# Second feed-forward layer of a two-layer diffusion block: its up projection as seven block products

## The chip, the cores and the metric

The kernel runs on one core of a Trainium2 chip. The metric is the device time of one execution in microseconds (us), the median of several. One core has a matrix engine (TensorE: PE for the products, PEld for the loading of its weights), a vector engine (VectorE, DVE), an activation engine (ScalarE, ACT), a general engine (GpSimd, POOL) and a queue engine that starts most transfers (SyncE, SP). Each runs its own program in order; they meet at semaphores.

## The reference

Two blocks, each a mixer and a gated convolutional feed-forward layer (FFN), on 1024 latent tokens and 256 context tokens of width 1024 in float32. What the change touches is the FFN of the second block, on the 1024 latent tokens alone:

```
def conv_ffn(h, w_up, conv_w, conv_b, w_down):
    gate, val = jnp.split(dwconv_centred(h @ w_up, conv_w, conv_b), 2, axis=-1)
    return (jax.nn.silu(gate) * val) @ w_down
...
xl = xl + g2 * conv_ffn(rmsnorm(xl, norm_ffn_w[i]) * (1 + sc2) + sh2, ffn_w_up[i], ...)
```

The convolution runs over three neighbouring tokens, each channel for itself. The hidden width is 2816, so `w_up` is 1024 x 5632 and `w_down` 2816 x 1024.

## The kernel before

Channels lie on the 128 partitions, tokens along the row. The hidden width is cut into FT = 22 tiles of 128 channels. One tile has a gate half and a value half; for each, 8 weight blocks of 128x128 (the width 1024 = KD x 128) are multiplied with 1024 tokens in two groups of 512. Every float32 product is made of three passes (`split_passes`, high x high, high x low, low x high), for which each operand is split into a rounded part (`_hi`) and a remainder (`_lo`). So one tile has 2 x 2 x 8 x 3 = 96 matmuls of 512 columns for the up projection, and its down projection has ND = 16 pieces (8 output blocks x 2 token groups) of 3 matmuls, 48 more.

The function `ffn` writes an order by hand for each engine; nothing is scheduled by a planner:

- SP loads the two halves of a tile's up weights (`up_raw`) and its down weights (`dn_raw`), 512 KB each.
- POOL splits them: `up_hi` (L1285) and `up_lo` (L1288) for each half, then `dn_hi` (L1294) and `dn_lo` (L1297), on 128x1024 each, two operands in the on-chip memory SBUF for the `_lo`.
- PE (L1317 for up, L1310 for down) runs the up products of tile f, and between them the down pieces of tile f-1, at steps given by a list `place`. A gate half fills banks 0 and 1 of the accumulators (PSUM), a value half banks 3 and 4; down pieces alternate between banks 6 and 7.
- ACT takes a half out of PSUM with the middle tap (`centre`, L1366), DVE adds the two outer taps (L1395, L1401), ACT applies Silu (L1376), DVE multiplies the halves (L1433), ACT rounds the product (`act_hi`, L1380) and DVE makes the remainder (`act_lo`, L1435).
- DVE adds each down piece to the residual (`add`, L1414). PE may begin piece j when the add of piece j-2 has ended, since there are two banks.

Ahead of the tiles `normalise` makes the normed activations: DVE multiplies by the inverse root (L279), ACT scales and shifts and rounds, and DVE makes the remainder (L288), eight blocks of 128x1024 each. PE's first tile takes each block as soon as it is there. The order of DVE inside a tile, and the down pieces on PE:

```
        def body(dve, f, s, with_down):
            if with_down:
                for j in range(in_gate):
                    add(f - 1, j)
            dve.wait_ge(lo_set, f + 1)
            convolve(f, 0)
            if with_down:
                for j in range(in_gate, ND):
                    add(f - 1, j)
            convolve(f, 1)
            ...
```

## Time and profile before

| what | value |
|---|---|
| median of 3 runs (lowest to highest) | 3511.73 us (3507.72 to 3512.95) |
| the profiled execution | 3508.97 us, its span on the core 3507.2 us |
| PE busy, share of the span | 3208.5 us, 91% |
| DVE, ACT, POOL busy | 2204.2, 984.5, 988.9 us |
| chain that ended last, largest parts | PE L1317 14%, PE L1310 7% of the span |
| L1317, three passes, both FFN layers | 652.9, 652.2 and 650.5 us busy, 1760 matmuls each |
| up weights, issue to landing | 88 transfers of 512 KB, median 3.5 us |

The span is the time from the first to the last instruction of the profiled execution; 1.8 us of its time lie around it. Busy time is the sum of the durations of an engine's instructions, and it includes time in which an instruction that has begun is held up. The second FFN fills the last fifth of the span.

### The profile page before, as it was taken

Reading aid. Unit: us, or ns where it says so; the run is one execution under the profiler, and the core shown is the slowest. Engines: PE = TensorE matmul, PEld = TensorE weight load, DVE = VectorE, ACT = ScalarE, POOL = GpSimd, SP = SyncE. Lnnn points to the kernel's source line nnn. Section 1 sums busy time; section 2 is a strip of 40 time slices with the busy share of each in tenths; the row PEclk is TensorE's granted clock in tenths of the full one; section 3 lists DMA queues with packets and bytes.
Section 4 is the critical chain, followed back from the end, with each engine's and each line's share of the span. In section 5 each row is a group of like instructions: output and inputs, shape, how many; then the busy total and the mean of one; then the engine's idle time right before and its main releaser. Section 6 shows DMA issues by size and latency. Waiting matters only on the chain. (4 is left out here: it accounts for less than half of the span.)

```text
span 3507.2 us, 53513 instructions
## 1 busy us (share of the span) xinstructions
PE 3208.5 (91%) x20022; PEld 2673.9 (76%) x20022; DVE 2204.2 (63%) x2995; ACT 984.5 (28%) x1504; POOL 988.9 (28%) x715
## 2 busy tenths in 40 slices
PE   5989988886899999999996879999998799999998
PEld 3879956665688888888885658878887688888886
DVE  7976067886366666666666256666663566666666
ACT  4111245544131111111112434444442312112111
POOL 1322145551222222222220032221212333333331
PEclk8999999998999999999998879999999899999999
DMA  4558120004111111111100200000002111111111
GB/s 194 193 177 292 68 77 2 2 2 158 38 47 38 36 37 40 36 36 36 36 30 14 72 9 5 5 6 10 2 13 84 55 42 54 48 42 54 48 46 56
DMA packets 64267, 196.35 MB, mean 56 GB/s; under 512 B 7680, under 2 KB 20864, under 8 KB 62848
## 3 DMA queue, kind: packets, MB, share of 16 engines
q1 hardware_dynamic: 47280, 163.83, 14.0%
q10 hardware_dynamic: 16848, 30.56, 2.6%
q8 instruction: 100, 1.64, 0.2%
q14 instruction: 39, 0.32, 0.0%
HBM read 175.49 MB, written 18.87 MB: 55 GB/s over the span
## 5 line engine op out<-in xcount | busy, mean ns | idle before, releaser
L1414 DVE SCALAR_TENSOR_TENSOR resid<-ps,mod,resid 128x512 f32<-128x512 f32 (+1 forms) x880 | 601.8, 697 | 471.5 <-PE ps L1310 471.3
L1317 PE MATMUL ps<-hf_hi,up_hi 128*128 128x512 f32 (+1 forms) x1760 | 652.9, 371 | 31.3 <-DVE hf_lo L288 22.3
L1317 PE MATMUL ps<-hf_lo,up_hi 128*128 128x512 f32 (+1 forms) x1760 | 652.2, 371 | 0.0
L1317 PE MATMUL ps<-hf_hi,up_lo 128*128 128x512 f32 (+1 forms) x1760 | 650.5, 370 | 0.0
L1285 POOL TENSOR_SCALAR up_hi<-up_raw 128x1024 fp32r<-128x1024 f32 x88 | 94.7, 1076 | 1161.0 <-PE ps L1317 1099.4
L1317 PEld LDWEIGHTS ps<-hf_hi,up_hi 128*128 128x128 f32 x1760 | 334.6, 190 | 87.6 <-issue 34.3
L1317 PEld LDWEIGHTS ps<-hf_hi,up_lo 128*128 128x128 f32 x1760 | 334.2, 190 | 56.5
L1317 PEld LDWEIGHTS ps<-hf_lo,up_hi 128*128 128x128 f32 x1760 | 334.8, 190 | 51.6
L1310 PE MATMUL ps<-act_hi,dn_hi 128*128 128x512 f32 (+1 forms) x880 | 333.1, 379 | 18.3 <-DVE act_lo L1435 16.1
L1366 ACT ACTIVATE conv<-ps,conv_w 128x1280 f32<-128x1280 f32 (+1 forms) x88 | 115.7, 1315 | 802.3 <-PE ps L1317 802.0
L1310 PE MATMUL ps<-act_lo,dn_hi 128*128 128x512 f32 (+1 forms) x880 | 326.7, 371 | 0.0
L1310 PE MATMUL ps<-act_hi,dn_lo 128*128 128x512 f32 (+1 forms) x880 | 325.6, 370 | 0.0
L820 POOL TENSOR_TENSOR k_decayed<-decay,qk 128x256 f32<-128x256 f32 (+1 forms) x240 | 194.1, 838 | 193.1 <-ACT decay L985 193.1
L131 DVE CUSTOM_DVE_ANT_0 ps<-adaw_ring,cond,adab 128x1024 f32<-128x1024 f32 x128 | 205.9, 1608 | 58.9 <-DMA adaw_ring<-in_adaw 48.5
L1310 PEld LDWEIGHTS ps<-act_hi,dn_hi 128*128 128x128 f32 x880 | 166.4, 189 | 71.0 <-DVE resid L1414 20.7
L1288 POOL TENSOR_TENSOR up_lo<-up_raw,up_hi 128x1024 fp32r<-128x1024 f32 x88 | 213.2, 2423 | 7.3
L2080 DVE TENSOR_TENSOR pt_lo<-ps,pt_hi 128x512 fp32r<-128x512 f32 (+1 forms) x192 | 114.5, 597 | 135.4 <-ACT pt_hi L1981 134.8
L1310 PEld LDWEIGHTS ps<-act_lo,dn_hi 128*128 128x128 f32 x880 | 166.9, 190 | 28.6
L1310 PEld LDWEIGHTS ps<-act_hi,dn_lo 128*128 128x128 f32 x880 | 166.5, 189 | 28.8
L649 PE MATMUL ps<-wvr_hi,h_hi 128*128 128x256 f32 x640 | 182.5, 285 | 4.2 <-ACTq L678 4.2
L649 PE MATMUL ps<-wvr_lo,h_hi 128*128 128x256 f32 x640 | 182.1, 284 | 0.0
L649 PE MATMUL ps<-wvr_hi,h_lo 128*128 128x256 f32 x640 | 182.0, 284 | 0.0
(239 smaller groups left out, 6590.5 us busy)
## 6 DMA issues: line engine op xcount, KB each, us to landing
up_raw<-in_up SPq DMA_DIRECT2D x88, 512.0 KB, 3.5
adaw_ring<-in_adaw SPq DMA_DIRECT2D x80, 512.0 KB, 4.0
dn_raw<-in_dn SPq DMA_DIRECT2D x44, 512.0 KB, 3.5
vr<-vr_out ACTq DMA_DIRECT2D x80, 128.0 KB, 3.7
adaw_first<-in_adaw SPq DMA_DIRECT2D x16, 512.0 KB, 21.8
wvr_raw<-in_wvr SPq DMA_DIRECT2D x8, 1024.0 KB, 7.3
x<-in_xT ACTq DMA_DIRECT2D x8, 640.0 KB, 16.9
r<-vr ACTq DMA_DIRECT2D x10, 512.0 KB, 3.8
```

The source lines that it names most:

```text
L131: return dve.tensor_tensor_reduce(junk, w, self.cond[:, j, :], 1.0, self.bias[:, n:n + 1], ALU.mult, ALU.add, self.c.mod[:, n, j:j + 1])
L649: mm = pe.matmul(c.ps[:, u % RING, 0:W], a[:, k, t * P:(t + 1) * P], b[:, s, k, :], start=(k == 0 and a is h_hi and b is w_hi), stop=(k == ...
L820: pool.tensor_tensor(kd[u % 2][:, lo * P:hi * P].rearrange("p (b t) -> p b t", t=P), e[:, u % 2, (LEVEL + lo) * P:(LEVEL + hi) * P].rearra ...
L1285: pool.tensor_scalar(up_hi[:, half, :, :], up_raw[:, half, :, :], 1.0, 1.0, ALU.mult, ALU.mult).then_inc(up_hi_set, 1)
L1288: pool.tensor_tensor(up_lo[:, half, :, :], up_raw[:, half, :, :], up_hi[:, half, :, :].bitcast(F32), ALU.subtract).then_inc(up_split, 1)
L1310: mm = pe.matmul(c.ps[:, 6 + j % 2, 0:w], a[:, s, m * P:(m + 1) * P], b[:, s, t:t + w], start=(a is dn_hi and b is act_hi), stop=(a is dn_lo))
L1317: mm = pe.matmul(c.psf[:, at:at + w], a[:, half, k, :], b[:, k, t:t + w], start=(k == 0 and a is up_hi and b is h_hi), stop=(k == KD - 1 a ...
L1366: act.activation(y[:, half, span], u(half), ACT.Identity, scale=cw[:, bass.ds(f * 8 + (half * 4 + 1), 1)], bias=cw[:, bass.ds(f * 8 + (hal ...
L1414: dve.scalar_tensor_tensor(resid[:, m, t:t + w], c.ps[:, 6 + j % 2, 0:w], c.mod[:, gate + m, cond[t]:cond[t] + 1], resid[:, m, t:t + w], A ...
L2080: dve.tensor_tensor(pt_lo[:, k0:k0 + w, at], c.psf[:, T_PS[n]:T_PS[n] + w * P].rearrange("p (k t) -> p k t", t=P), pt_hi[:, k0:k0 + w, at] ...
```

## The change

The second FFN no longer calls `normalise` and `ffn`, but a function of its own, `seven_ffn`. The first FFN stays. The up projection of one tile is seen as a 2 x 2 block matrix of weights (gate and value half, times the first and second half of the 1024 input channels, HK = 4 blocks each) times a 2 x 2 block matrix of activations (halves of the channels times halves of the tokens, HALF = 512). Strassen's identity in Winograd's form makes the four output blocks from seven block products in place of eight, from four weight sums, four activation differences and seven sums of products:

- the operands of the seven products of the activations (`x_hi`, `x_lo`, 128 x 7 x 4 x 512) are made once ahead of the tiles: DVE scales (`scale`, 16 instructions), POOL takes differences (`differences`, 16 instructions), ACT rounds and DVE makes the remainders (`low`, 28 instructions);
- for each tile POOL makes four sums of weight blocks and splits seven operands of 128x512 into a ring of three places (`slots`); it splits operand n when the product three before has ended. The split of the down weights stands after the third operand, and there is one place for it where there were two;
- PE runs seven products of 4 x 3 matmuls (84 in place of 96) into banks 4, 0, 5, 3, 1, 4, 2, and the down pieces of the tile before at the steps 13 to 20 and 24 to 27 of 28;
- DVE makes seven sums of products in PSUM or SBUF (`mixed`), between the adds and the taps, and begins a tile with the value half of the tile before (`value`).

The core of the diff (declarations, the SP queue, the norm on ACT and the last tile are left out):

```diff
+HALF = SEQ // 2
+HK = KD // 2
+SEVEN_BANKS = (4, 0, 5, 3, 1, 4, 2)
+SLOTS = 3
+def seven_ffn(c, block, layer, resid, wup_d, conv_d, wdn_d, out_d, holes):
...
+    room = list(range(13, 21)) + list(range(24, 28))
+    place = [room[j * len(room) // ND] for j in range(ND)]
+    def bank(n):
+        return c.ps[:, SEVEN_BANKS[n], :]
+    def u(half):
+        return c.psf[:, 2 * half * BANK:2 * half * BANK + SEQ]
+    def units(eng, body):
+        body(eng, 0, 0, False)
+        with eng.Fori(0, (FT - 1) // SLOTS, 1) as i:
+            for s in range(SLOTS):
+                body(eng, i * SLOTS + (s + 1), s + 1, True)
+    @block.gpsimd
+    def _(pool):
+        a11, a12 = raw[:, 0, 0:HK, :], raw[:, 0, HK:KD, :]
+        a21, a22 = raw[:, 1, 0:HK, :], raw[:, 1, HK:KD, :]
+        def split(f, s, n, source):
+            w_hi, w_lo = slots[(s + n) % SLOTS]
+            pool.wait_ge(product_done, f * 7 + (n + 1))
+            pool.nop(nofuse=True)
+            pool.tensor_scalar(w_hi, source, 1.0, 1.0, ALU.mult, ALU.mult).then_inc(w_hi_set, 1)
+            pool.wait_ge(w_hi_set, f * 7 + (n + 1))
+            pool.tensor_tensor(w_lo, source, w_hi.bitcast(F32), ALU.subtract).then_inc(w_split, 1)
+        def differences():
+            for i in range(HK):
+                pool.wait_ge(scaled, 2 * i + 2)
+                pool.wait_ge(x_split, i + 1)
+                pool.tensor_tensor(w11[:, i, :], w12[:, i, :], w11[:, i, :], ALU.subtract).then_inc(differed, 1)
+            for i in range(HK):
+                pool.wait_ge(scaled, 2 * (HK + i) + 2)
+                pool.wait_ge(differed, i + 1)
+                pool.tensor_tensor(e2[:, i, :], w22[:, i, :], w11[:, i, :], ALU.subtract).then_inc(differed, 1)
+            for i in range(HK):
+                pool.wait_ge(differed, HK + i + 1)
+                pool.tensor_tensor(w12[:, i, :], w22[:, i, :], w12[:, i, :], ALU.subtract).then_inc(differed, 1)
+            for i in range(HK):
+                pool.wait_ge(x_split, HK + i + 1)
+                pool.wait_ge(differed, 2 * HK + i + 1)
+                pool.tensor_tensor(w21[:, i, :], e2[:, i, :], w21[:, i, :], ALU.subtract).then_inc(differed, 1)
+        def body(pool, f, s, with_down):
+            pool.wait_ge(up_in[0], f * 16 + 16)
+            split(f, s, 0, a11)
+            split(f, s, 1, a12)
+            pool.wait_ge(up_in[1], f * 16 + 16)
+            pool.nop(nofuse=True)
+            pool.tensor_tensor(s1[:, :, :], a21, a22, ALU.add).then_inc(sums, 1)
+            pool.wait_ge(sums, f * 4 + 1)
+            pool.tensor_tensor(s2[:, :, :], s1[:, :, :], a11, ALU.subtract).then_inc(sums, 1)
+            pool.wait_ge(sums, f * 4 + 2)
+            if not with_down:
+                pool.wait_ge(summed, 1)
+            split(f, s, 2, s2[:, :, :])
+            pool.tensor_tensor(a21, a11, a21, ALU.subtract).then_inc(sums, 1)
+            pool.wait_ge(w_split, f * 7 + 3)
+            pool.tensor_tensor(s2[:, :, :], a12, s2[:, :, :], ALU.subtract).then_inc(sums, 1)
+            if with_down:
+                pool.wait_ge(dn_in, f * 16)
+                pool.wait_ge(dn_done, f * ND + (1 - ND))
+                pool.wait_ge(x_split, 7 * HK)
+                pool.nop(nofuse=True)
+                pool.tensor_scalar(dn_hi[:, :], dn_raw[:, :], 1.0, 1.0, ALU.mult, ALU.mult).then_inc(dn_hi_set, 1)
+                pool.wait_ge(dn_hi_set, f)
+                pool.tensor_tensor(dn_lo[:, :], dn_raw[:, :], dn_hi[:, :].bitcast(F32), ALU.subtract
+                                   ).then_inc(dn_split, 1)
+            else:
+                differences()
+            split(f, s, 3, s1[:, :, :])
+            pool.wait_ge(sums, f * 4 + 4)
+            split(f, s, 4, s2[:, :, :])
+            split(f, s, 5, a21)
+            split(f, s, 6, a22)
...
+    @block.tensor
+    def _(pe):
+        for h in range(2):
+            mm = pe.matmul(c.ps[:, h, :], c.ones[:, :], c.total[:, CTX + h * HALF:CTX + (h + 1) * HALF],
+                           start=True, stop=True)
+        mm.then_inc(summed, 1)
+        pe.sem_inc(product_done, SLOTS)
+        pe.sem_inc(dn_done, 1)
+        def down(f, j):
+            m, t = j // 2, j % 2 * HALF
+            pe.wait_ge(added, f * ND + (j + 1))
+            for a, b in split_passes(dn_hi, dn_lo, act_hi, act_lo):
+                mm = pe.matmul(c.ps[:, 6 + j % 2, :], a[:, m * P:(m + 1) * P], b[:, t:t + HALF],
+                               start=(a is dn_hi and b is act_hi), stop=(a is dn_lo))
+            mm.then_inc(dn_done, 1)
+        def body(pe, f, s, with_down):
+            j = 0
+            for n in range(7):
+                w_hi, w_lo = slots[(s + n) % SLOTS]
+                pe.wait_ge(w_split, f * 7 + (n + 1))
+                if n == 5:
+                    pe.wait_ge(p1_set, f + 1)
+                if with_down and n == 0:
+                    pe.wait_ge(mixed, f * 7 - 2)
+                if with_down and n == 1:
+                    pe.wait_ge(u_read, f * 2 - 1)
+                if with_down and n == 3:
+                    pe.wait_ge(u_read, f * 2)
+                for k in range(HK):
+                    if not with_down:
+                        pe.wait_ge(x_split, n * HK + k + 1)
+                    for a, b in split_passes(w_hi, w_lo, x_hi, x_lo):
+                        mm = pe.matmul(bank(n), a[:, k, :], b[:, n, k, :], start=(k == 0 and a is w_hi and b is x_hi),
+                                       stop=(k == HK - 1 and a is w_lo))
+                    if k == HK - 1:
+                        mm.then_inc(product_done, 1)
+                    while with_down and j < ND and place[j] == n * HK + k:
+                        if j == 0:
+                            pe.wait_ge(lo_set, f)
+                            pe.wait_ge(dn_split, f)
+                        down(f - 1, j)
+                        j += 1
...
+    @block.scalar
...
+        def value(f):
+            act.wait_ge(mixed, f * 7 + 7)
+            centre(f, 1)
+        def rounded(f, after_downs):
+            act.wait_ge(mult_set, f + 1)
+            if after_downs:
+                act.wait_ge(dn_done, f * ND + 1)
+            act.activation(act_hi[:, :], y[:, 0, :], ACT.Copy).then_inc(hi_set, 1)
+        def body(act, f, s, with_down):
+            if with_down:
+                value(f - 1)
+            act.wait_ge(product_done, f * 7 + (1 + SLOTS))
+            act.activation(ua[:, :], bank(0), ACT.Copy).then_inc(p1_set, 1)
+            if with_down:
+                rounded(f - 1, True)
+                act.wait_ge(lo_set, f)
+            act.wait_ge(mixed, f * 7 + 4)
+            centre(f, 0)
+            act.wait_ge(u_read, f * 2 + 1)
+            act.activation(y[:, 0, :], y[:, 0, :], ACT.Silu).then_inc(silu_set, 1)
...
+    @block.vector
...
+        def scale(k):
+            first, second = (w11, w12) if k < HK else (w21, w22)
+            dve.scalar_tensor_tensor(first[:, k % HK, :], resid[:, k, CTX:CTX + HALF], gain[:, k, 0:1],
+                                     rstd[:, 0:HALF], ALU.mult, ALU.mult).then_inc(scaled, 1)
+            dve.scalar_tensor_tensor(second[:, k % HK, :], resid[:, k, CTX + HALF:T], gain[:, k, 0:1],
+                                     rstd[:, HALF:SEQ], ALU.mult, ALU.mult).then_inc(scaled, 1)
+        def low(n, k, source, bias):
+            dve.wait_ge(x_hi_set, n * HK + k + 1)
+            dve.scalar_tensor_tensor(x_lo[:, n, k, :], source[:, k, :], bias, x_hi[:, n, k, :].bitcast(F32),
+                                     ALU.add, ALU.subtract).then_inc(x_split, 1)
...
+        def value(f):
+            dve.wait_ge(product_done, f * 7 + (7 + SLOTS))
+            dve.tensor_tensor(bank(6), ua[:, :], bank(6), ALU.subtract).then_inc(mixed, 1)
+            taps(f, 1)
+            dve.wait_ge(silu_set, f + 1)
+            dve.wait_ge(u_read, f * 2 + 2)
+            dve.tensor_tensor(y[:, 0, :], y[:, 0, :], y[:, 1, :], ALU.mult).then_inc(mult_set, 1)
+            dve.wait_ge(hi_set, f + 1)
+            dve.tensor_tensor(act_lo[:, :], y[:, 0, :], act_hi[:, :].bitcast(F32), ALU.subtract
+                              ).then_inc(lo_set, 1)
+        def body(dve, f, s, with_down):
+            j = 0
+            def adds(step):
+                nonlocal j
+                while with_down and j < ND and place[j] < step:
+                    if j == 0:
+                        dve.wait_ge(added, f * ND - (ND - 2))
+                    add(f - 1, j)
+                    j += 1
+            if with_down:
+                value(f - 1)
+            dve.wait_ge(p1_set, f + 1)
+            dve.wait_ge(product_done, f * 7 + (2 + SLOTS))
+            dve.tensor_tensor(bank(1), bank(1), ua[:, :], ALU.add).then_inc(mixed, 1)
+            dve.wait_ge(product_done, f * 7 + (3 + SLOTS))
+            dve.wait_ge(mixed, f * 7 + 1)
+            dve.tensor_tensor(ua[:, :], bank(2), ua[:, :], ALU.add).then_inc(mixed, 1)
+            adds(16)
+            dve.wait_ge(product_done, f * 7 + (4 + SLOTS))
+            dve.wait_ge(mixed, f * 7 + 2)
+            dve.tensor_tensor(ub[:, :], bank(3), ua[:, :], ALU.add).then_inc(mixed, 1)
+            adds(20)
+            dve.wait_ge(product_done, f * 7 + (5 + SLOTS))
+            dve.wait_ge(mixed, f * 7 + 3)
+            dve.tensor_tensor(bank(4), bank(4), ub[:, :], ALU.add).then_inc(mixed, 1)
+            adds(21)
+            taps(f, 0)
+            dve.wait_ge(product_done, f * 7 + (6 + SLOTS))
+            dve.tensor_tensor(ua[:, :], bank(5), ua[:, :], ALU.add).then_inc(mixed, 1)
+            dve.wait_ge(mixed, f * 7 + 5)
+            dve.tensor_tensor(bank(3), bank(3), ua[:, :], ALU.add).then_inc(mixed, 1)
+            adds(28)
...
+def latent_ffn(c, a, layer, resid, out_d):
+    spare = c.at("w7_spare", 141, [P, KD, T], F32R)
+    holes = [(spare[:, q:q + HK, 0:P], spare[:, q:q + HK, P:2 * P]) for q in (0, HK)]
+    with c.stage() as block:
+        seven_ffn(c, block, layer, resid, a[f"up{layer}"], a[f"conv{layer}"], a[f"dn{layer}"], out_d, holes)
...
-        ffn_layer(c, a, 1, resid, CTX, out)
+        latent_ffn(c, a, 1, resid, out)
```

POOL's program inside the loop over tiles, before (the second half of one turn; `up_raw` and `dn_raw` are the loaded weights):

```order
L1283 REGISTER_ALU
L1285 TENSOR_SCALAR up_hi_18606<-up_raw_18604 128x1024
L1288 TENSOR_TENSOR up_lo_18607<-up_raw_18604,up_hi_18606 128x1024
L1283 REGISTER_ALU
L1285 TENSOR_SCALAR up_hi_18606<-up_raw_18604 128x1024
L1288 TENSOR_TENSOR up_lo_18607<-up_raw_18604,up_hi_18606 128x1024
L1294 TENSOR_SCALAR dn_hi_18609<-dn_raw_18608 128x1024
L1297 TENSOR_TENSOR dn_lo_18610<-dn_raw_18608,dn_hi_18609 128x1024
```

The same engine after the change, from the third operand of a tile to the fourth (`w_sum_409` and `w_sum_410` are the sums `s1` and `s2`; `w_hi`/`w_lo` and `w_spare` are places of the ring):

```order
L1523 REGISTER_ALU
L1525 TENSOR_SCALAR w_hi_18534<-w_sum_410_18525 128x512
L1527 TENSOR_TENSOR w_lo_18535<-w_sum_410_18525,w_hi_18534 128x512
L1560 TENSOR_TENSOR up_raw_18523<-up_raw_18523 128x512
L1562 TENSOR_TENSOR w_sum_410_18525<-up_raw_18523,w_sum_410_18525 128x512
L1565 REGISTER_ALU
L1568 TENSOR_SCALAR dn_hi_18527<-dn_raw_18526 128x1024
L1570 TENSOR_TENSOR dn_lo_18528<-dn_raw_18526,dn_hi_18527 128x1024
L1523 REGISTER_ALU
L1525 TENSOR_SCALAR w_spare_18510<-w_sum_409_18524 128x4x128
L1527 TENSOR_TENSOR w_spare_18510<-w_sum_409_18524,w_spare_18510 128x4x128
```

Two weight sums and the split of the down weights now stand between the splits of the third and of the fourth operand, and PE needs the fourth for its fourth product.

DVE's program before, around the taps of the gate half (`resid` is the residual, `conv` the convolved halves):

```order
L1413 REGISTER_ALU
L1414 SCALAR_TENSOR_TENSOR resid_9871<-ps,mod_55,resid_9871 128x512
L1423 REGISTER_ALU
L1392 ISA
L1395 ISA
L1395 SCALAR_TENSOR_TENSOR conv_18603<-ps,conv_w_18605,conv_18603 128x1023
L1401 ISA
L1401 SCALAR_TENSOR_TENSOR conv_18603<-ps,conv_w_18605,conv_18603 128x1023
L1413 REGISTER_ALU
L1414 SCALAR_TENSOR_TENSOR resid_9871<-ps,mod_55,resid_9871 128x512
```

The same place after the change, from the sum with the fifth product on (`u_a` and `u_b` are running sums):

```order
L1806 TENSOR_TENSOR ps<-ps,u_b_18530 128x512
L1753 REGISTER_ALU
L1754 SCALAR_TENSOR_TENSOR resid_9871<-ps,mod_55,resid_9871 128x512
L1759 ISA
L1760 ISA
L1760 SCALAR_TENSOR_TENSOR conv_18522<-ps,conv_w_18531,conv_18522 128x1023
L1764 ISA
L1764 SCALAR_TENSOR_TENSOR conv_18522<-ps,conv_w_18531,conv_18522 128x1023
L1809 REGISTER_ALU
L1810 TENSOR_TENSOR u_a_18529<-ps,u_a_18529 128x512
L1812 TENSOR_TENSOR ps<-ps,u_a_18529 128x512
```

Sums with products now stand ahead of the gate's taps and behind them, and the last five adds of the tile follow behind these sums.

## Rows read from the trace of the kernel before

**Rows 1.** Windows: us; busy of PE, PEld, DVE, ACT, POOL; PE clock; DMA share, GB/s.
```profile
2826.00:2858.70 32.70, 32.70 (x146) 26.97 (x145) 20.70 (x23) 7.12 (x7) 11.17 (x7) 1.00 0.15 49
```

**Rows 2.** The chain that ended last: start, us, what; same piece, 19 tiles apart.
```profile
2825.69 8.84 PE ps L1317 x39
...
3446.69 8.84 PE ps L1317 x39
```

**Rows 3.** Groups of instructions, shapes apart, window 2791 to 3479 (busy us, mean ns).
```profile
L1414 DVE SCALAR_TENSOR_TENSOR resid<-ps,mod,resid 128x512 f32<-128x512 f32 x335 | 247.2, 750 | 206.2 <-PE ps L1310 206.2
...
L1297 POOL TENSOR_TENSOR dn_lo<-dn_raw,dn_hi 128x1024 fp32r<-128x1024 f32 x21 | 67.3, 3207 | 1.8
...
L1401 DVE SCALAR_TENSOR_TENSOR conv<-ps,conv_w,conv 128x1023 f32<-128x1023 f32 x43 | 55.2, 1283 | 6.2 <-DVE conv L1395 6.1
...
L1366 ACT ACTIVATE conv<-ps,conv_w 128x1024 f32<-128x1024 f32 x43 | 52.0, 1210 | 347.6 <-PE ps L1317 347.5
...
L1294 POOL TENSOR_SCALAR dn_hi<-dn_raw 128x1024 fp32r<-128x1024 f32 x21 | 22.0, 1047 | 0.0
```

**Rows 4.** Groups, shapes apart, whole span: 128x512 forms of POOL and DVE.
```profile
L1742 POOL TENSOR_TENSOR wuq_lo<-wuq,wuq_hi 128x512 fp32r<-128x512 f32 x8 | 10.2, 1280 | 0.7
...
L1739 POOL TENSOR_SCALAR wuq_hi<-wuq 128x512 fp32r<-128x512 f32 x8 | 5.0, 620 | 0.0
...
L1034 DVE SCALAR_TENSOR_TENSOR ps<-ps,gate_log 128x512 f32<-128x512 f32 x18 | 12.6, 700 | 11.9 <-ACT gate_log L971 11.9
```

**Rows 5.** Timeline of the norm and behind it: start, us, engine, line.
```profile
2753.43 5.16 DVE L279 TENSOR_TENSOR wide<-resid,rstd 128x1024 f32<-128x1024 f32 x2 [5.72 <-ACT rstd L248]
...
2757.61 3.20 POOL L1288 TENSOR_TENSOR up_lo<-up_raw,up_hi 128x1024 fp32r<-128x1024 f32 x1
...
2759.08 2.81 DVE L288 TENSOR_TENSOR hf_lo<-full,hf_hi 128x1024 fp32r<-128x1024 f32 x1 [0.49 <-ACT hf_hi L259]
...
2760.78 2.01 POOL L1294 TENSOR_SCALAR dn_hi<-dn_raw 128x1024 fp32r<-128x1024 f32 x1
...
2771.88 1.22 DVE L279 TENSOR_TENSOR wide<-resid,rstd 128x1024 f32<-128x1024 f32 x1
...
2793.78 2.39 POOL L1297 TENSOR_TENSOR dn_lo<-dn_raw,dn_hi 128x1024 fp32r<-128x1024 f32 x1
```

**Rows 6.** Timeline of one tile's end in the loop.
```profile
3022.42 2.40 POOL L1288 TENSOR_TENSOR up_lo<-up_raw,up_hi 128x1024 fp32r<-128x1024 f32 x1
...
3024.10 1.28 DVE L1401 SCALAR_TENSOR_TENSOR conv<-ps,conv_w,conv 128x1023 f32<-128x1023 f32 x1 [0.15 <-DVE conv L1395]
...
3025.42 1.49 DVE L1433 TENSOR_TENSOR conv<-conv 128x1024 f32<-128x1024 f32 x1
3025.92 3.25 POOL L1297 TENSOR_TENSOR dn_lo<-dn_raw,dn_hi 128x1024 fp32r<-128x1024 f32 x1
3027.02 1.06 ACT L1380 ACTIVATE act_hi<-conv 128x1024 fp32r<-128x1024 f32 x1 [4.51 <-DVE conv L1433]
3028.11 2.14 DVE L1435 TENSOR_TENSOR act_lo<-conv,act_hi 128x1024 fp32r<-128x1024 f32 x1 [1.21 <-ACT act_hi L1380]
```

**Rows 7.** Timeline of the tail: PE's first down matmul, DVE's last add.
```profile
3486.68 0.80 PE L1310 MATMUL ps<-act_hi,dn_hi 128*128 128x512 f32 x1 [7.32 <-DVE act_lo L1435]
...
3502.86 0.75 DVE L1414 SCALAR_TENSOR_TENSOR resid<-ps,mod,resid 128x512 f32<-128x512 f32 x1 [0.33 <-PE ps L1310]
```

**Rows 8.** Windows with waits of PE: attention, then the second FFN's tile 1.
```profile
2210.00:2216.00 6.00, 3.79 (x24) 3.00 (x22) 4.42 (x7) 2.71 (x5) 3.13 (x4) 1.00 0.00 0
2216.00:2222.00 6.00, 6.00 (x49) 5.87 (x49) 2.05 (x3) 0.94 (x4) 2.32 (x3) 1.00 0.01 3
2281.00:2287.00 6.00, 3.79 (x21) 2.96 (x19) 4.41 (x8) 2.87 (x5) 2.93 (x3) 0.97 0.00 1
2287.00:2293.00 6.00, 5.51 (x25) 5.22 (x25) 2.33 (x4) 0.47 (x2) 2.50 (x4) 0.50 0.02 5
2792.00:2796.00 4.00, 4.00 (x12) 3.19 (x11) 2.61 (x3) 1.21 (x2) 3.92 (x3) 0.59 0.50 147
```

147 lines of the change are left out of this document (added).

## Prediction

> **What bounds the kernel now.** I read the windows of one tile first: between 2826.00 and 2858.70 PE is busy for 32.70 of 32.70 us at clock 1.00, DVE for 20.70, POOL for 11.17, ACT for 7.12 [rows 1]. The second FFN is bound by PE alone. The chain that ended last agrees; the same piece of it comes back 19 tiles later, (3446.69 - 2825.69) / 19 = 32.68 us for a tile of 144 matmuls, 0.227 us for a matmul [rows 2]. Fewer matmuls are worth their full time only as long as nothing else is late. So the question is whether POOL and DVE, which get more to do, stay behind PE, and for that their durations and their order count, not their shares.
>
> **What is removed.** 12 of 144 matmuls in each tile: 132 x 0.227 = 29.96 us, 2.72 us less a tile if PE never waits, 57 us over 21 tiles.
>
> **Prices.** POOL on 128x512: 1.28 us with two operands, 0.62 us with one [rows 4]; a split is 0.62 + 0.08 (between the two, as 3024.80+1.04 to 3025.92 is in the loop) + 1.28 = 1.98 us. The down split is 1.05 [rows 3] + 0.08 + 2.39 us when nothing holds it up [rows 5]. An add is 0.75 us [rows 3], 0.69 where two follow each other. A sum of a product with a running sum on DVE has no row of this shape and operands in PSUM; the nearest is 0.70 us [rows 4], and where it needs the one before, another 0.15 us, as between two taps [rows 6]. A tap is 1.28, `centre` 1.21 [rows 3], `act_hi` 1.06 us [rows 6]. DVE with two SBUF operands on 128x1024 takes 1.22 us [rows 5]; half of it, 0.61, is my price for 128x512 (0.70 at most, by the other row).
>
> **Who holds up whom.** DVE's `hf_lo` began at 2759.08 and took 2.81 us, not 1.22: POOL's `up_lo` ran until 2760.81, and `hf_lo` ended 1.08 us behind it, at 2761.89; POOL's next instruction, 1.05 us by itself, began at 2760.78 and took 2.01, to 0.90 behind the end of `hf_lo` [rows 3, 5]. In the loop `dn_lo` takes 3.25 us because the product of the halves (L1433) runs first, and `act_lo` 2.14 because `dn_lo` still runs [rows 6]; the mean of 21 `dn_lo` is 3207 ns [rows 3]. The taps, which read one operand from PSUM, are 1.28 us beside `up_lo` and do not stretch its 2.40 [rows 6]. I read this as an exclusion: a DVE instruction with two SBUF operands and a POOL instruction run one after the other, taking turns. The Trainium skill says so (SBUF — State Buffer, "Who interferes with whom": the second to issue "fully blocks", also where DVE has two SBUF inputs and the other reads SBUF); this trace agrees by 2.81 against 1.22 us. Were the port shared and each slowed, `act_lo` below would run beside the split that PE waits for and put it off by up to its own 1.22 us, 24 us in all; I take turns, since the ends fall 1.08 us apart.
>
> **One tile after the change**, from the end of the last matmul of the seventh product (t = 0), handing over in 0.1 to 0.2 us:
> - PE: one down piece (0.68), then three products (36 x 0.227 = 8.17). It wants the fourth at 8.85.
> - POOL: the third operand's place is free at 0.2, split to 2.2; two sums to 3.4 and 4.8 (0.08 between); down split to 5.9 and, `dn_lo`, 8.3 (its single place is free, since the last down piece ended at 0.7). Then the fourth operand.
> - DVE: the last add ends at 1.6, the seventh sum at 2.2; `centre` on ACT to 3.5; two taps with 0.15 between to 6.2. The product of halves asks at 6.3, `dn_lo` is running: it goes from 8.3 to 9.5. POOL's next waits for that: 9.5 to 10.1, then 10.2 to 11.5. `act_hi` to 10.7; `act_lo` waits for POOL and goes from 11.5 to 12.7.
> - PE begins the fourth product at 11.5: **waits 2.65 us**. Two steps (1.36) later, at 12.9, the first down piece finds `act_lo` ready.
> - DVE makes two sums by 14.0, then follows PE's pieces; the tenth add ends at 24.7, and the sum of the fifth product at 25.3 (the product ended at 22.6). ACT's `centre` 25.5 to 26.7, taps to 29.3, two sums to 30.7, and only then the twelfth add, to 31.4. PE stands at the fourteenth piece from 29.9: it **waits 1.6 us**.
> - PE ends the seventh product at 34.2: 29.96 + 2.65 + 1.6.
>
> The clock: in attention PE stood still for 2.21 us of 2210 to 2216 and kept clock 1.00 in the six us behind; the same pause in 2281 to 2287 brought 0.50 in the next six. Where it fell in this FFN, 12 matmuls fit into 4.00 us at 0.59 where 17.6 would: 1.3 us lost [rows 8]. A pause of 2.65 us in every tile will sometimes do it. I take 0.55 us a tile, between nothing and 1.8 (a fall each time, some of it longer): 34.8 us, 2.1 more than before.
>
> **Ahead of the tiles.** `rstd` is ready at 2753.43 as before [rows 5]. From there to the last remainder DVE has 16 + 28 = 44 instructions with two SBUF operands, 44 x 0.62 = 27.3 us. POOL begins its splits before; what it has left until then is 28 instructions with two operands (16 differences, and the weight sums and remainders of tile 0 and of the first two operands of tile 1) x 1.28 = 35.8, and 8 roundings x 0.62 = 5.0. In turns, with always one of the two waiting, that is 68.1 us: 2821.5. Running freely it would be POOL's 40.8 with the last remainders behind it, 44 to 50. I take turns: the rows of the norm show them. One step of PE more (1.1 us at the low clock) ends tile 0 at 2822.6. Before, tile 1 began at 2791.2, so this is the price that the loop would have to earn.
>
> Tile 1 waits for DVE: four sums, `centre`, taps and a fifth sum are 6.6 us before its first product, since nothing of tile 0 could run earlier; 34.2 + 6.1 = 40.3 us.
>
> **The tail.** From the seventh product's end the chain above without POOL: sum 2.2, `centre` 3.5, taps 6.2, product 7.5, `act_hi` 8.7, `act_lo` 9.9; before it was 7.32. The 16 pieces and adds then take 3503.61 - 3486.68 = 16.9 us and the store 3507.2 - 3503.61 = 3.6, as before [rows 7]. Together 30.5.
>
> Transfers cost nothing: the bytes are the same; SP issues a tile's second half when the seventh split has ended (18.5 in the walk), it lands some 4 us later (22.5) and POOL reads it at 29.4. Without these 7 us POOL's third operand would be late.
>
> **The sum**, on the profiled execution: 2822.6 + 40.3 + 20 x 34.8 + 30.5 = 3589.4 for the span, 82 us more than 3507.2. The profiled execution took 3508.97, the median of the runs is 3511.73; 82 above that is **3594 us**.
>
> **Rivals.**
> - *No exclusion that matters* (POOL and DVE hardly meet). The fourth operand is ready at 10.4, PE waits 1.6 and again 1.6: 33.15 a tile; tile 0 ends at 2798, tile 1 takes 37. 2798 + 37 + 663 + 30.5 = 3528.5, median 3533. Against it: all rows of the norm [rows 5].
> - *The clock falls in most tiles.* 20 x 1.2 more: 3618. For it: one of two pauses did it [rows 8]; against it: the pause stands between long full stretches.
> - *Faster: PE never waits in the loop.* Then 20 x 29.96 in place of 696 and a tile 1 of 36: 3488 for the span, median 3492. It needs POOL's fourth operand by 8.85 where I have 11.5, and the twelfth add by 29.9 where I have 31.4. The point from which it decides: (3507.2 - 2822.6 - 40.3 - 30.5) / 20 = 30.7 us a tile; the two waits together must be under 0.7 us. Since POOL's own chain with no meeting at all is 10.4 us long, this wants POOL's instructions 15% shorter than the rows and no exclusion.
> - *Nothing comes of it* (within 0.2%, 7 us, which is about what a measurement of this kernel can tell from no change): a tile of 30.4 to 31.1 us, a balance that no row asks for.
>
> **How the numbers follow.** The forecast 0.55; clock in most tiles 0.24; no exclusion 0.13; faster 0.05; no change 0.03. Slower is 0.92. The forecast alone holds 3570 to 3610: POOL's prices for 512 columns by 0.08 us each way change ten instructions of the chain and the ahead part by 10 to 15 us. The range goes down to the case without exclusion, 3533, and up past the clock's, 3618, with POOL slower by 0.04 us in each: 3530 to 3630.
>
> **What would show it.** In the loop of the changed kernel: a PE matmul of the fourth product that waits 2 to 3.5 us for POOL's `w_lo`; `dn_lo` and the product of halves one behind the other, with the latter at 2 us or more; a wait of 1 to 2 us before the fourteenth down piece, released by an add; 84 + 48 matmuls in 34 to 36 us. Ahead: remainders on DVE of 1.2 to 1.9 us each in place of 0.7, and the last one near 2821. I am wrong if the fourth product starts on time, if the norm's remainders are short, or if DVE is not behind at the fifth product.

## The result and the profile after

The changed kernel takes 3589.2 us (median of 4 runs, 3586.74 to 3589.63) against 3511.96 for the one before: ratio 1.0221, 95% interval 1.0203 to 1.0239. It is slower by 77 us; forecast were 3594 and the range 3530 to 3630. The profiled execution took 3586.74 us. One execution of an experiment below, e4, took 4666.87 us at a granted clock of 0.629, where its others had 0.953 to 0.957; nothing here explains it, and e4's median leaves it out. The first lines of its page:

```profile
span 3585.0 us, 54165 instructions
...
PE 3183.7 (89%) x19758; PEld 2636.1 (74%) x19758; DVE 2349.5 (66%) x3178; ACT 968.6 (27%) x1517; POOL 1291.5 (36%) x1039
```

PE executes fewer matmuls and the span is 78 us longer, so the loss is time in which PE waits or runs at the lower clock. The windows of the changed kernel (columns as in [rows 1]): the norm from `rstd` to the last remainder; one tile; a stretch in which the clock fell; the tail.

```profile
2755.40:2815.90 60.50, 31.25 (x82) 19.29 (x82) 60.50 (x45) 18.24 (x29) 53.19 (x37) 0.63 0.08 26
...
3148.80:3183.30 34.50, 30.50 (x132) 24.62 (x132) 25.66 (x30) 5.11 (x5) 23.65 (x21) 1.00 0.13 46
...
2974.40:2978.40 4.00, 4.00 (x13) 3.09 (x12) 2.61 (x4) 0.00 (x0) 3.47 (x4) 0.57 0.10 40
...
3555.00:3585.10 30.10, 16.49 (x53) 9.50 (x51) 18.79 (x23) 2.26 (x2) 3.38 (x2) 0.83 0.34 140
```

Beside [rows 1] the tile has 132 matmuls for 144, and lasts 34.50 us for 32.70. PE, which never stood still there, now does so for 4 us. The list of PE's waits in the loop (us in total, times, longest) says for what:

```profile
PE ps L1602 <- DVE resid L1754: 34.0, 20, 1.7
PE ps L1623 <- POOL w_spare L1527: 29.8, 13, 2.3
PE ps L1623 <- POOL w_lo L1527: 16.1, 7, 2.3
```

Two waits in each of 20 tiles: 2.3 us for the remainder of a weight operand from POOL, 1.7 us for an add from DVE, 79.9 us in all. In PE's timeline the first of the rows below is the first matmul of tile 1, the last the first matmul of a fourth product, and those between stand around the fourteenth down piece:

```profile
2823.36 0.80 PE L1623 MATMUL ps<-x_hi,w_spare 128*128 128x512 f32 x1 [6.50 <-DVE u_a L1810]
...
3167.32 0.39 PE L1602 MATMUL ps<-act_hi,dn_lo 128*128 128x512 f32 x1
3169.41 0.50 PE L1602 MATMUL ps<-act_hi,dn_hi 128*128 128x512 f32 x1 [1.70 <-DVE resid L1754]
3169.75 0.40 PE L1602 MATMUL ps<-act_lo,dn_hi 128*128 128x512 f32 x1
...
3183.56 0.50 PE L1623 MATMUL ps<-x_hi,w_hi 128*128 128x512 f32 x1 [2.29 <-POOL w_lo L1527]
```

**Why 2.29.** POOL's timeline up to that matmul shows its work ahead of the fourth operand, one behind the other without a gap:

```profile
3177.07 1.05 POOL L1568 TENSOR_SCALAR dn_hi<-dn_raw 128x1024 fp32r<-128x1024 f32 x1
3178.20 2.40 POOL L1570 TENSOR_TENSOR dn_lo<-dn_raw,dn_hi 128x1024 fp32r<-128x1024 f32 x1
3180.57 1.59 POOL L1525 TENSOR_SCALAR w_hi<-w_sum 128x512 fp32r<-128x512 f32 x1
3182.24 1.26 POOL L1527 TENSOR_TENSOR w_lo<-w_sum,w_hi 128x512 fp32r<-128x512 f32 x1
```

The rounding in the third row takes 1.59 us where 0.62 is its price [rows 4]. DVE's timeline has the reason: the product of the halves asked at 3178.86, waited for `dn_lo` and ended at 3181.68, and the rounding ended 0.48 us behind it. `act_lo` then took turns with `w_lo`:

```profile
3178.86 2.82 DVE L1775 TENSOR_TENSOR conv<-conv 128x1024 f32<-128x1024 f32 x1
3182.89 1.70 DVE L1777 TENSOR_TENSOR act_lo<-conv,act_hi 128x1024 fp32r<-128x1024 f32 x1 [1.21 <-ACT act_hi L1688]
```

**Why 1.70.** DVE, from the gate half's second tap to the twelfth and thirteenth add (merged in the last row). The fourteenth piece waits for the twelfth, which had to stand behind the two sums; by the trace it ended at 3169.36, and PE went on at 3169.41:

```profile
3166.09 1.28 DVE L1764 SCALAR_TENSOR_TENSOR conv<-ps,conv_w,conv 128x1023 f32<-128x1023 f32 x1 [0.16 <-DVE conv L1760]
3167.29 0.68 DVE L1810 TENSOR_TENSOR u_a<-ps,u_a 128x512 f32<-128x512 f32 x1
3168.01 0.70 DVE L1812 TENSOR_TENSOR ps<-ps,u_a 128x512 f32<-128x512 f32 x1
3168.62 1.40 DVE L1754 SCALAR_TENSOR_TENSOR resid<-ps,mod,resid 128x512 f32<-128x512 f32 x2
```

**Ahead of the tiles.** `rstd` was ready 2 us later than in the profiled execution before [rows 5]; from there DVE never rests. The first row is the first scaling; the others are groups of four remainders:

```profile
2755.39 0.95 DVE L1717 SCALAR_TENSOR_TENSOR w<-resid,gain,rstd 128x512 f32<-128x512 f32 x1 [5.60 <-ACT rstd L1646]
...
2792.83 6.77 DVE L1729 TENSOR_TENSOR x_lo<-w,x_hi 128x512 fp32r<-128x512 f32 x4
2799.52 5.46 DVE L1724 SCALAR_TENSOR_TENSOR x_lo<-w,mod,x_hi 128x512 fp32r<-128x512 f32 x4
```

Beside the first group POOL makes four differences, and each engine gets one instruction done in (2799.52 - 2792.83) / 4 = 1.67 us:

```profile
2792.32 6.73 POOL L1545 TENSOR_TENSOR w<-e,w 128x512 f32<-128x512 f32 x4
```

**Where 77.8 us of span went.** Tile 1 began at 2823.36 in place of 2791.2: 32.2 (2 of them the later start). From there to PE's wait in the tail 732.6 in place of 688.2: 44.4. The wait in the tail (before PE's row at 3564.98) is 9.00 in place of 7.32: 1.7. What follows: -0.5 [rows 7]. The 44.4 are -57.2 for the 252 matmuls removed, +79.9 for the waits, and 21.7 for the clock (5 falls of 1.6 in the loop, and tile 1) and for what a wait costs beyond its record (40 x 0.26, below).

### The profile page after: what moved, and what is told of

The parts are those of the page before. It is cut to its first block and busy times, and to the rows that moved or that the text cites. A ratio compares the mean times of both kernels' runs of the same rounds, so it can differ in the third digit from the quotient of the medians.

```text
span 3585.0 us, 54165 instructions
## 1 busy us (share of the span) xinstructions
PE 3183.7 (89%) x19758; PEld 2636.1 (74%) x19758; DVE 2349.5 (66%) x3178; ACT 968.6 (27%) x1517; POOL 1291.5 (36%) x1039
## 3 DMA queue, kind: packets, MB, share of 16 engines
q1 hardware_dynamic: 47280, 163.83, 13.6%
## 5 line engine op out<-in xcount | busy, mean ns | idle before, releaser
L1414 DVE SCALAR_TENSOR_TENSOR resid<-ps,mod,resid 128x256 f32<-128x256 f32 x528 | 342.1, 661 | 259.9 <-PE ps L1310 259.6
L1317 PE MATMUL ps<-hf_hi,up_hi 128*128 128x512 f32 (+1 forms) x1056 | 377.0, 357 | 16.0 <-DVE hf_lo L288 11.3
L1317 PE MATMUL ps<-hf_lo,up_hi 128*128 128x512 f32 (+1 forms) x1056 | 376.9, 357 | 0.0
L1317 PE MATMUL ps<-hf_hi,up_lo 128*128 128x512 f32 (+1 forms) x1056 | 375.2, 355 | 0.0
L1623 PE MATMUL ps<-x_hi,w_spare 128*128 128x512 f32 x824 | 299.9, 403 | 66.6 <-POOL w_spare L1527 37.7
L1754 DVE SCALAR_TENSOR_TENSOR resid<-ps,mod,resid 128x512 f32<-128x512 f32 x352 | 258.0, 750 | 112.3 <-PE ps L1602 111.0
L1623 PEld LDWEIGHTS ps<-x_hi,w_spare 128*128 128x128 f32 x824 | 159.3, 193 | 113.4 <-POOL w_spare L1527 43.6
L1310 PE MATMUL ps<-act_hi,dn_hi 128*128 128x256 f32 x528 | 193.6, 367 | 10.4 <-DVE act_lo L1435 8.8
L1310 PE MATMUL ps<-act_lo,dn_hi 128*128 128x256 f32 x528 | 188.6, 357 | 0.0
L1310 PE MATMUL ps<-act_hi,dn_lo 128*128 128x256 f32 x528 | 187.7, 355 | 0.0
L1602 PE MATMUL ps<-act_hi,dn_hi 128*128 128x512 f32 x352 | 144.0, 409 | 44.8 <-DVE resid L1754 35.7
```

What stands on the lines that cost most here:

```text
L1310: mm = pe.matmul(c.ps[:, 6 + j % 2, 0:w], a[:, s, m * P:(m + 1) * P], b[:, s, t:t + w], start=(a is dn_hi and b is act_hi), stop=(a is dn_lo))
L1317: mm = pe.matmul(c.psf[:, at:at + w], a[:, half, k, :], b[:, k, t:t + w], start=(k == 0 and a is up_hi and b is h_hi), stop=(k == KD - 1 a ...
L1414: dve.scalar_tensor_tensor(resid[:, m, t:t + w], c.ps[:, 6 + j % 2, 0:w], c.mod[:, gate + m, cond[t]:cond[t] + 1], resid[:, m, t:t + w], A ...
L1602: mm = pe.matmul(c.ps[:, 6 + j % 2, :], a[:, m * P:(m + 1) * P], b[:, t:t + HALF], start=(a is dn_hi and b is act_hi), stop=(a is dn_lo))
L1623: mm = pe.matmul(bank(n), a[:, k, :], b[:, n, k, :], start=(k == 0 and a is w_hi and b is x_hi), stop=(k == HK - 1 and a is w_lo))
L1754: dve.scalar_tensor_tensor(resid[:, m, t:t + HALF], c.ps[:, 6 + j % 2, :], c.mod[:, gate + m, 0:1], resid[:, m, t:t + HALF], ALU.mult, ALU ...
```

## The experiments

Each is an edit of the changed kernel (3589.2 us), timed in five rounds beside the kernel before, whose median in them was 3510.9 to 3511.3. "Tile" is the mean distance from one `act_lo` to the next over 18 tiles, in brackets its value where the clock did not fall; the last column counts the falls in the loop behind tile 1.

| run | us | against the changed kernel | tile, us | falls |
|---|---|---|---|---|
| changed kernel | 3589.2 | | 34.87 (34.5) | 5 |
| e1 adds ahead of sums | 3569.8 | -19.4 | 34.15 (33.2) | 11 |
| e2 weight sums first | 3564.7 | -24.5 | 33.80 (33.8) | 0 |
| e3 value half in PSUM | 3561.5 | -27.7 | 33.55 (33.5) | 0 |
| e4 down split later | 3579.5 | -9.7 | 34.50 (34.3) | 2 |
| e5 rstd in PSUM | 3577.5 | -11.7 | 34.88 (34.5) | 5 |
| e6 differences on DVE | 3579.7 | -9.5 | 34.87 (34.5) | 5 |
| e7 = e1 + e2 + e3 | 3513.0 | -76.2 | 31.24 (31.2) | 0 |
| e8 = e7 + e5 + e6 | 3499.4 | -89.8 | 31.27 (31.2) | 0 |
| e9 = e8, pieces placed anew | 3505.7 | -83.5 | 31.50 (31.5) | 0 |
| e10 = e9 without e3 | 3551.8 | -37.4 | 33.98 (32.5) | 18 |
| e11 = e9 + e4's order | 3473.7 | -115.5 | 29.94 (29.9) | 0 |

**e1.** DVE's order:

```
             taps(f, 0)
+            adds(26)
             dve.wait_ge(product_done, f * 7 + (6 + SLOTS))
```

> One edit on the changed kernel: in a tile, DVE makes the twelfth to fourteenth adds right behind the gate half's taps, ahead of the two sums with the sixth and seventh product, not behind them. Theory (DVE's order makes the wait of 1.70 us before the fourteenth down piece): the wait goes to 0 to 0.3 us, the tile from 34.94 to 33.1 to 33.4 us, the time to 3589 - 20 x 1.6 = 3557 us (3550 to 3565); the two sums end 2 us later, at about 33.0 of the tile, and nothing waits for that. Rival (the two PSUM banks for the pieces and the 0.75 us of an add set that wait, not the order): the wait stays at 1.7 us, 3589. Rival (the sums are needed early): the wait moves to the next tile's first product, 3580 to 3590.

The waits in the loop of e1:

```profile
PE ps L1623 <- POOL w_spare L1527: 29.8, 13, 2.3
PE ps L1623 <- POOL w_lo L1527: 16.1, 7, 2.3
PE ps L1602 <- DVE resid L1754: 7.9, 21, 0.4
```

The wait for the add fell from 34.0 to 7.9 us, so DVE's order made it and not the two banks. The time missed its range of 3550 to 3565: 26 us of waiting went and 19.4 of time, since the clock fell 11 times and not 5. A tile with a fall is 34.8 us long and one without 33.2.

**e2.** POOL's order:

```
+            pool.tensor_tensor(a21, a11, a21, ALU.subtract).then_inc(sums, 1)
+            pool.wait_ge(w_split, f * 7 + 2)
+            pool.tensor_tensor(a12, a12, s2[:, :, :], ALU.subtract).then_inc(sums, 1)
             ...
             split(f, s, 2, s2[:, :, :])
-            pool.tensor_tensor(a21, a11, a21, ALU.subtract).then_inc(sums, 1)
-            pool.tensor_tensor(s2[:, :, :], a12, s2[:, :, :], ALU.subtract).then_inc(sums, 1)
...
-            split(f, s, 4, s2[:, :, :])
+            split(f, s, 4, a12)
```

> One edit on the changed kernel: POOL makes the third and fourth weight sum of a tile (1.27 us each) ahead of the third operand's split, in time in which it stood idle (2.85 us there), the fourth in the place of one quarter of the weights and not in the place of the second sum; the reload of that half waits for the fifth split. Theory (POOL's order makes the wait of 2.30 us before the fourth product): that wait goes to 0 to 0.3 us; some 0 to 0.3 us may come up at the first down piece; the tile 32.2 to 32.6, the time 3589 - 20 x 2.4 = 3541 us (3533 to 3550). Rival (the ring of three operands is too small): the fourth operand still comes late, over 1 us of the wait is left, 3565 or more. Rival (the later reload is felt): POOL waits for a transfer ahead of the first operand's split, and PE with it.

```profile
PE ps L1602 <- DVE resid L1754: 35.7, 21, 1.7
PE ps L1602 <- DVE act_lo L1777: 31.7, 20, 1.6
```

No wait for POOL is left: with the same ring of three the fourth operand was in time. But 1.6 us came up at the first down piece, which waits for `act_lo`. I had put 0 to 0.3 there, so the time lies above its range of 3533 to 3550. The product of the halves now met the fourth split in place of `dn_lo`, and `act_lo` the fifth (e2, DVE):

```profile
3165.30 2.29 DVE L1775 TENSOR_TENSOR conv<-conv 128x1024 f32<-128x1024 f32 x1
3168.80 1.71 DVE L1777 TENSOR_TENSOR act_lo<-conv,act_hi 128x1024 fp32r<-128x1024 f32 x1 [1.22 <-ACT act_hi L1688]
```

**e3.** The value half through PSUM (`v` is banks 1 and 2; ACT makes the last column; PE's fourth product waits for the product of the halves):

```
-            dve.tensor_tensor(y[:, 0, :], y[:, 0, :], y[:, 1, :], ALU.mult).then_inc(mult_set, 1)
+            dve.tensor_tensor(v[:, 0:SEQ - 1], y[:, 0, 0:SEQ - 1], u(1)[:, 1:SEQ], ALU.mult).then_inc(mult_set, 1)
...
-            dve.tensor_tensor(act_lo[:, :], y[:, 0, :], act_hi[:, :].bitcast(F32), ALU.subtract
+            dve.tensor_tensor(act_lo[:, :], v, act_hi[:, :].bitcast(F32), ALU.subtract
```

> One edit on the changed kernel: the value half's second tap leaves its sum in PSUM, the product of the halves reads it there and is written to PSUM, act_lo is made from there (the last column by ACT); the same arithmetic, but in the loop no DVE instruction has two SBUF operands. Theory (the product of the halves and POOL's down split take turns at a port, and each is put off): the product takes 1.2 to 1.3 us in place of 2.80, act_lo 1.2 to 1.3 in place of 1.70, POOL's two roundings of 1.6 us become 0.62, the wait before the fourth product goes from 2.30 to 1.2 to 1.4, the time to 3589 - 20 x 1.0 = 3569 us (3562 to 3573, at its low end if the clock falls less often). Rival (the order alone makes the wait; the stretched rows are only the way in which the waits are recorded): the wait stays at 2.2 to 2.4, 3585 to 3592. Rival (a bank held longer is felt): PE waits for the product of the halves, 3589 or more.

The groups of e3 (busy us, mean ns):

```profile
L1781 DVE TENSOR_TENSOR ps<-conv,ps 128x1023 f32<-128x1023 f32 x18 | 22.1, 1229 | 1.9
L1783 DVE TENSOR_TENSOR act_lo<-ps,act_hi 128x1024 fp32r<-128x1024 f32 x18 | 22.0, 1224 | 26.6 <-ACT act_hi L1694 26.6
```

The product takes 1.23 us, where 2.80 was its mean in the changed kernel; `act_lo` 1.22 and not 1.70. POOL's rounding behind `dn_lo` is back at 0.62, and PE's wait for the fourth operand at 1.3 (26.5 us in 20). Same arithmetic, same order, one operand elsewhere (and the last column on ACT): the exclusion at SBUF is shown, and it was 1.0 us of the 2.3. The other 1.3 stay without it; e2 shows that order removes them. The time came out 0.5 us below its range of 3562 to 3573, and the clock did not fall.

**e4.** `split(f, s, 3, ...)` ahead of the down split.

> One edit on the changed kernel: POOL splits the down weights behind the fourth operand's split, not ahead of it. Theory (POOL has too much to do between the seventh product and the first down piece, and the port adds to it): the wait before the fourth product goes, but the down split then ends at about 11.4 of the tile and act_lo, which must wait for it, at 12.5, where the first down piece wants them at 10.2: a wait of 1.3 to 2.4 us there in place of 2.30, the time 3575 to 3592 us. Rival (only what stands ahead of the fourth split matters): the wait goes and none comes, 3541 us.

```profile
PE ps L1602 <- DVE act_lo L1777: 42.3, 20, 2.1
PE ps L1602 <- DVE resid L1754: 34.0, 20, 1.7
```
```profile
3178.51 3.23 DVE L1777 TENSOR_TENSOR act_lo<-conv,act_hi 128x1024 fp32r<-128x1024 f32 x1 [1.22 <-ACT act_hi L1688]
```

The wait went to the first down piece, 2.1 us, as expected: `act_lo` now meets `dn_lo` and takes 3.23 us (second fence: e4's DVE). Moving one step does not help as long as POOL's two sums stand there too and `act_lo` has to take turns with what is put behind.

**e5 and e6.** The norm. e5 writes `rstd` to PSUM, e6 gives POOL's 16 differences to DVE:

```
-        act.activation(rstd[:, :], rstd[:, :], ACT.Exp, scale=-0.5).then_inc(rstd_set, 1)
+        act.activation(u(1), rstd[:, :], ACT.Exp, scale=-0.5).then_inc(rstd_set, 1)
```
```
-                pool.tensor_tensor(w11[:, i, :], w12[:, i, :], w11[:, i, :], ALU.subtract).then_inc(differed, 1)
...
+            difference(w11[:, i, :], w12[:, i, :], w11[:, i, :])
```

> One edit on the changed kernel, ahead of the tiles: ACT writes rstd to two PSUM banks, so that the norm's 16 scaling instructions on DVE read one operand from SBUF and one from PSUM. Theory (DVE's two-operand instructions and POOL's take turns at a port, and that makes the 60.4 us from rstd to the last remainder): the 16 take 0.7 us each where now up to 1.75, POOL's weight sums beside them 1.27 in place of 1.7, the stretch 51 to 54 us, the time 3580 to 3583 us. Rival (the stretch is a chain of results that DVE and POOL hand each other; no port): the scalings keep their mean, 3588 to 3590.

> One edit on the changed kernel, ahead of the tiles: the 16 differences of activations are made on DVE, between its remainders, not on POOL. Theory (one port; a POOL instruction of 1.27 us holds it in full, one of DVE's for about 0.40 to 0.45 of its 0.67): 16 x 1.27 = 20.3 us leave POOL, DVE has 60 x 0.67 = 40.2 us and stands behind POOL's 12 two-operand instructions and 8 roundings for about 15 more, 55 us in place of 60.4; 3583 to 3586 us. Rival (each engine's instructions cost the same whoever makes them, DVE is the longer one): 44 x 1.38 + 16 x 0.67 = 71 us, 3599.

From the first scaling to the last remainder e5 takes 50.9 us and e6 52.7, for 60.4. In e5 a scaling lasts 0.73 to 0.75 us beside any of POOL's instructions:

```profile
2757.56 0.74 DVE L1719 SCALAR_TENSOR_TENSOR w<-resid,gain,ps 128x512 f32<-128x512 f32 x1
```

In e6 the stretch became shorter with the work on the engine that was busy all the time: what filled DVE was waiting for POOL. The times came out 2.5 and 3.3 us below the ranges expected.

**e7 and e8.** e1, e2 and e3 together, then all five.

> The three edits in the loop together: the twelfth to fourteenth adds ahead of the two sums, the third and fourth weight sum ahead of the third split, the value half through PSUM. Seen so far: the first left 0.38 us of the wait at the fourteenth piece, the second took the 2.30 us before the fourth product and brought 1.6 at the first down piece, where act_lo came late after the product of the halves had taken 2.25 and act_lo itself 1.71. Theory (that new wait is the port's, 1.0 + 0.5 us in that row): with the value half in PSUM it goes; 0.4 us a tile are left, a tile of 132 matmuls takes 30.4 us, the clock does not fall; 3589 - 20 x 4.5 = 3499 us (3494 to 3508), 0.1 to 0.5% below the kernel before. Rival (the new wait is the chain's own, centre, taps, product, act_hi, act_lo): over 1 us of it stays, 3520 or more.

> All five edits: the three in the loop, rstd in PSUM, the differences on DVE. Theory: as with the three in the loop, and the stretch ahead of the tiles shorter: DVE has 60 instructions of 0.67 to 0.7 us, POOL's 20 us of weight work runs beside the 16 scalings and stands in the way of the others for some 8 us: 47 to 50 us in place of 60.4, so 10 to 13 us less than with the three alone, 3487 us (3480 to 3497). Rival (tile 0 is bound by PE's steps at the low clock once the remainders come faster): only 5 us less, 3494.

```profile
PE ps L1605 <- DVE resid L1760: 7.6, 20, 0.4
PE ps L1605 <- DVE act_lo L1783: 0.9, 5, 0.2
```

The 1.6 us of e2 at the first piece are gone, so they were the exclusion's and not the chain's own. So little waiting is left in e7, and yet a tile is 31.24 us long and not 30.4; e7 misses its range (3494 to 3508) and ties with the kernel before (ratio 1.0002, 0.9993 to 1.0011). What I had missed is in PE's timeline around the fourteenth piece of e7:

```profile
3103.13 0.39 PE L1605 MATMUL ps<-act_hi,dn_lo 128*128 128x512 f32 x1
3103.89 0.50 PE L1605 MATMUL ps<-act_hi,dn_hi 128*128 128x512 f32 x1 [0.38 <-DVE resid L1760]
3104.23 0.39 PE L1605 MATMUL ps<-act_lo,dn_hi 128*128 128x512 f32 x1
```

From start to start it is 0.76 us, not 0.23, and then 0.34: the recorded wait of 0.38 costs 0.53 + 0.11 = 0.64. In the changed kernel the 1.70 cost (3169.41 - 3167.32 - 0.23) + 0.11 = 1.97. A pause costs 0.26 us beyond its record. e7 has three in a tile, 0.64, 0.44 at the first piece and 0.18 at the fourth product; 29.96 + 1.26 = 31.22. e8 takes 13.6 us less than e7, and its norm 46.7 us, where 10 to 13 and 47 to 50 were expected; its time lies 2.4 us above its range, since e7 did. It is below the kernel before (0.9965, 0.9951 to 0.9978).

**e9 and e10.** All pauses should go with another placement:

```
-    room = list(range(13, 21)) + list(range(24, 28))
-    place = [room[j * len(room) // ND] for j in range(ND)]
+    place = [14, 14, 15, 15, 16, 16, 17, 18, 18, 19, 19, 20, 24, 25, 27, 27]
...
-            adds(20)
+            adds(19)
...
-            adds(21)
+            adds(20)
             taps(f, 0)
-            adds(26)
+            adds(21)
```

> The five edits and one more, in the order of the down pieces and adds: 12 pieces behind the fourth to sixth product's steps (from the fifteenth step on) and the last four behind steps 25, 26 and, two, 28; DVE makes the sum of the fifth product before the adds of the pieces around it, and the eleventh and twelfth add ahead of the sums with products 6 and 7. In the run with the five edits 31.3 us a tile were 29.96 for 132 matmuls, 0.65 around the wait at the fourteenth piece, 0.44 at the first piece and 0.18 at the fourth product, each with the slower matmuls behind it. Theory (nothing else limits the loop): all three go, 30.0 to 30.2 us a tile, 20 x 1.2 = 24 us less than with the five: 3475 us (3470 to 3482), 1.0% below the kernel before. Rival (POOL, with 24.6 of 30 us, or a transfer is the next limit): 0.5 us a tile or more come back elsewhere, 3485 or more.

> As the run with the new placement, but the value half stays in SBUF, so that the product of the halves and act_lo have two SBUF operands again. It tells what the port is worth once the order is right. Theory (the port puts act_lo off by about 1.2 us, of which the placement can hide 0.4): 0.6 to 1.0 us a tile at the first down piece, 12 to 20 us more than with the value half in PSUM: 3487 to 3495 us. Rival (with the order right the port no longer matters): the same within 4 us.

e9 fell to its rival: no down piece waits any more, but the fourth product does again, 1.3 us for POOL. One down piece fewer now lies between the end of a tile's sixth product and the next tile's fourth, so POOL has 0.7 us less for its three splits, four sums and the down split. The pause of 0.64 us at the fourteenth piece, which lay in the same stretch, is gone too: with the 0.18 us that e7 had left, 0.18 + 0.68 + 0.64 = 1.50 us, against some 1.53 by which the fourth product now starts late (1.42 to its first matmul and 0.11 behind it).

```profile
PE ps L1605 <- POOL w_spare L1529: 16.4, 13, 1.3
PE ps L1605 <- POOL w_lo L1529: 8.8, 7, 1.3
```

e10 put the two SBUF operands back: 46 us more than e9, where I expected 12 to 20, and at another place than I expected, the fourth product. The wait is 2.24 us (44.8 in 20); a tile without a fall is 1.0 us longer, and the clock falls 18 times.

```profile
PE ps L1602 <- POOL w_spare L1526: 29.1, 13, 2.2
PE ps L1602 <- POOL w_lo L1526: 15.7, 7, 2.3
```

**e11.** e9 with the fourth split ahead of the down split, the order that failed in e4:

> The run with the new placement, and POOL splits the down weights behind the fourth operand's split. In that run PE never waited at a down piece, but 1.30 us before every fourth product: from the end of the sixth product POOL has the second split, four sums, the third split, the down split and the fourth split, 1.9 + 5.1 + 2.0 + 3.5 + 1.9 = 14.4 us, PE 2.7 + four pieces of 0.68 + 8.2 = 13.6. Theory: the fourth operand is ready 3.5 us sooner, at 10.9; the down split ends at 14.4 and the first piece wants it at 13.6 + 2.0 = 15.6, so nothing waits: 30.0 to 30.2 us a tile where it is 31.5, 20 x 1.35 = 27 us less, 3479 us (3474 to 3486), 0.9% below the kernel before. Rival (act_lo, no longer held by the order, or a later operand of POOL's becomes the limit): over 0.5 us a tile comes back, 3489 or more.

A tile's rows in the chain that ended last, 20 tiles apart:

```profile
2836.11 2.72 PE ps L1605 x12
...
3435.13 2.72 PE ps L1605 x12
```

(3435.13 - 2836.11) / 20 = 29.95 us, and 132 x 0.227 = 29.96. PE has no wait left between 2830 and 3440, and the time came out where it was expected (3474 to 3486, 0.3 us below its low end). 3473.7 us is 0.9891 of the kernel before (0.9874 to 0.9909): the seven products are worth their full 2.73 us a tile once nobody is late, 57 us over 21 tiles, of which the longer way to tile 1 takes some 20 (57.2 - 37.6; tile 1 begins at 2811.05 in place of 2791.2).

## Why the prediction was right, point by point

- **The tile** was forecast at 34.8 us and is 34.87. Its parts partly make up for each other: the wait at the fourth product 2.29 for 2.65, the one at the fourteenth piece 1.70 for 1.6, the clock 0.4 for 0.55, and 0.54 for two pauses beyond their record, a term that the sum did not have. That the total is met so closely is partly luck.
- **Who is late.** Both places and both causes held. Order and exclusion were named for the first: e2 and e3 show that each is a part of it. e1 shows the second.
- **The exclusion** was read from [rows 3, 5]; e3, e5 and e10 show it by taking it away or putting it back. The rival that the port is shared and each engine slowed did not come: `w_lo` took 1.26 us with `act_lo` waiting beside it, no more than its price. The Trainium skill (SBUF — State Buffer, "Who interferes with whom") says that a DVE instruction with at most one SBUF input does not meet POOL's. e3 agrees: 1.23 us with one of the two operands in PSUM, against 2.80. The Trainium skill (same page, "SBUF: two separate sides") also says that the one that starts first has the port for the whole instruction. Here that holds only nearly: POOL got its turn every 1.67 us, where each engine's instructions by themselves follow one another at 1.23 (POOL, the sums behind tile 0) and 0.60 us (DVE in e6), 1.83 together.
- **The stretch ahead** is the term that was mis-sized: 68.1 us forecast, 60.4 measured. POOL's instructions there are 28 x 1.27 + 8 x 0.62 = 40.5 us; that leaves (60.4 - 40.5) / 44 = 0.45 for one of DVE's, not 0.62. By the pair it is 1.67 - 1.27 = 0.40. The two agree: eight of the 44 ran at 0.66 us each while POOL stood still for DVE's results, and (8 x 0.66 + 36 x 0.40) / 44 = 0.45. By these sums the rest of DVE's instruction, some 0.2 us, lies beside POOL's next.
- **Tile 1 and tail.** PE's wait before tile 1 was to be 6.6 us and is 6.50 (the prediction's sum counts 6.1 of it and does not say why). The tail's wait came out 0.9 shorter than the walk's 9.9.
- **The sum:** tile 1 began 5.3 us sooner than the prediction's 2822.6 + 6.1 (-7.7 for the norm, +2.0 for the later start, the rest small), from there to the wait in the tail it took 2.4 us more (732.6 for 34.2 + 696), and the tail 1.5 less (29.0 for 30.5). That makes the 4.4 us by which the span, 3585.0, is below 3589.4.
- **The rivals.** No exclusion (33.15 a tile) is close to what e3 measured, 33.5, with the exclusion taken out of the loop. "Faster" needed a tile under 30.7 us, which was put as under 0.7 us of waits. e7 has 0.43 us of recorded waits a tile and just ties at 31.24: the pauses cost more than their record, and the way to tile 1 and the tail cost less than forecast.

## What to carry to other kernels

Work that is taken from the engine that sets the pace is worth nothing until the helpers deliver on time: walk one period with every engine's queue in order, and look for what stands ahead of the instruction that the pace-setter waits for. A single reordering mostly moves the wait to the next consumer (e2, e4, e9), so test the repairs together: in the loop e11 needed three orders, a placement and one operand in PSUM. Where DVE and POOL both work on two SBUF operands, count on them taking turns (here 1.67 us for a pair of 128x512), and put one operand of DVE's into PSUM where a bank is free.
